# Doubling levels of triangular inverses computed on two diagonal halves, with the level masks moved to GpSimd

## The reference

```python
def step(s, inp):
    r_t, w_t, k_t, v_t, kk_t, a_t = inp
    s_kk = jnp.einsum("bhvk,bhk->bhv", s, -kk_t)
    s = (s * w_t[:, :, None, :]
         + s_kk[..., None] * (kk_t * a_t)[:, :, None, :]
         + v_t[..., None] * k_t[:, :, None, :])
    y = jnp.einsum("bhvk,bhk->bhv", s, r_t)
    return s, y
```

## Time and profile before

| what | value |
|---|---|
| median of 3 runs | 2468.97 us (2467.76 to 2470.97) |
| the profiled execution: its time | 2468.69 us |
| the profiled execution: its span, first to last instruction | 2466.9 us |
| PE, DVE, ACT, POOL busy | 98%, 68%, 51%, 22% of the span |
| mean granted clock of TensorE | 0.993 of full speed |
| the levels, first copy of `p` to the last addition | 196.0 to 270.4 us of the span |

### The profile page before, as it was taken

How to read it: one execution, slowest core, us unless ns; L and a number is a source line. 1 busy time by engine, 2 the same in 40 slices (tenths; PEclk the granted TensorE clock), 3 DMA queues, 4 the chain that set the end, 5 groups by cost and what they waited for, 6 DMA issues and landing times.

```text
span 2466.9 us, 42599 instructions
## 1 busy us (share of the span) xinstructions
PE 2406.5 (98%) x16775; PEld 2183.0 (88%) x16775; DVE 1682.1 (68%) x3026; ACT 1261.8 (51%) x2689; POOL 541.0 (22%) x423
## 2 busy tenths in 40 slices
PE   7999999999999999999999999999999999999997
PEld 6888989998789999999888888789999999888886
DVE  4737345446669767887777556659776888777556
ACT  6542335445555544445555555545455455555554
POOL 3640224546178300000000002358500000000000
PEclk9999999999999999999999999999999999999999
DMA  5320145564145666666777665235666666787664
GB/s 179 121 87 17 36 153 169 188 188 143 49 156 171 186 181 194 195 195 193 241 245 224 195 211 151 90 113 168 183 187 185 195 193 193 227 247 237 195 199 145
DMA packets 148069, 421.00 MB, mean 171 GB/s; under 512 B 15904, under 2 KB 49056, under 8 KB 147488
## 3 DMA queue, kind: packets, MB, share of 16 engines
q1 hardware_dynamic: 144080, 405.34, 53.2%
q0 software_dynamic: 2192, 8.99, 1.0%
q10 hardware_dynamic: 1600, 3.96, 0.5%
HBM read 400.40 MB, written 17.83 MB: 170 GB/s over the span
## 4 chain that ended last, share of the span: by engine, by line
PE 92%; DVE 4%; ACT 2%; DMA 1%; issue 0%; POOL 0%; ACTq 0%; DVEq 0%
PE pb L436 91%; PE pb L445 1%; ACT arena L1135 1%; DVE arena L1618 1%; DVE arena L1621 0%; ACT L1135 0%; DVE arena L1767 0%; DMA raw<-in_vT 0%; DMA H<-in_x 0%; ACT hi L1123 0%; DVE H L1618 0%; DVE sm L1932 0%; DVE arena L2062 0%; DVE arena L1791 0%; DMA raw<-in_w_out 0%
## 5 line engine op out<-in xcount | busy, mean ns | idle before, releaser
L1123 ACT CAST hi<-raw 128x512 fp32r<-128x512 f32 x1402 | 819.2, 620 | 376.4 <-PE pb L436 192.5
L436 PE MATMUL pb<-HTh,hi 128*128 128x256 f32 (+1 forms) x2968 | 858.9, 289 | 2.6 <-POOL lo L2341 1.9
L436 PE MATMUL pb<-HTh,lo 128*128 128x256 f32 (+1 forms) x2968 | 842.2, 284 | 0.0
L436 PE MATMUL pb<-HTl,hi 128*128 128x256 f32 (+1 forms) x2968 | 842.2, 284 | 0.0
L2341 POOL TENSOR_TENSOR lo<-raw,hi 128x512 fp32r<-128x512 f32 x383 | 520.2, 1382 | 564.1 <-ACT hi L1123 564.1
L1628 DVE TENSOR_TENSOR lo<-raw,hi 128x1024 fp32r<-128x1024 f32 x464 | 565.3, 1218 | 85.7 <-ACT hi L1123 85.5
L436 PEld LDWEIGHTS pb<-HTh,hi 128*128 128x128 f32 x2968 | 569.7, 192 | 7.2 <-issue 2.7
L436 PEld LDWEIGHTS pb<-HTl,hi 128*128 128x128 f32 x2968 | 570.1, 192 | 0.9
L436 PEld LDWEIGHTS pb<-HTh,lo 128*128 128x128 f32 x2968 | 569.6, 192 | 0.0
L436 PE MATMUL pb<-hi,WH 128*128 128x512 f32 x1112 | 433.6, 390 | 4.3 <-DVE WL L2305 4.3
L436 PE MATMUL pb<-lo,WH 128*128 128x512 f32 x1112 | 433.2, 390 | 0.0
(11 more groups left out here) (196 smaller groups left out, 2166.0 us busy)
## 6 DMA issues: line engine op xcount, KB each, us to landing
raw<-in_uT SPq DMA_DIRECT2D x256, 512.0 KB, 3.6
raw<-in_vT SPq DMA_DIRECT2D x256, 512.0 KB, 4.2
raw<-in_w_ffn_in SPq DMA_DIRECT2D x44, 512.0 KB, 4.0
raw<-in_wq SPq DMA_DIRECT2D x32, 512.0 KB, 3.6
wk<-kept SPq DMA_DIRECT2D x128, 128.0 KB, 3.8
raw<-in_w_in SPq DMA_DIRECT2D x24, 512.0 KB, 3.8
raw<-in_w_ffn_out SPq DMA_DIRECT2D x22, 512.0 KB, 4.4
raw<-in_w_gate SPq DMA_DIRECT2D x16, 512.0 KB, 3.3
```

The source lines that it names most:

```text
L436: return e.matmul(o, l, r, start=start, stop=stop)
L1123: e.copy(u.hi[k], u.half[k]).then_inc(*s.up("hi", ("hi", g)))
```

## The change

For blocks 1 and 2 and levels 1 to 5 (`halved`), each matmul of 128x128 is replaced by two of 64x64 on the diagonal quarters. The bank index `q` then no longer stands for four heads but for a half (partitions 0 to 63 or 64 to 127) of all 8 heads, and the matmuls of the two halves alternate. ACT's copies and DVE's additions go by halves too: 64 partitions by 8x64 elements instead of 128 by 4x128. PE's order within a level becomes p, x_up, xt_up, each whole, with a wait for both copies of `p` ahead of `x_up`; this holds for all levels and blocks, the last level and block 0 too. The masks of blocks 1 and 2 go from DVE to POOL, which makes each as soon as both parts of `p` have been computed; POOL does them behind gate unit 7, in its program order. Level 6 and block 0 keep their matmuls, and block 0 its masks on DVE.

```diff
+    def part_of(self, i, lv, k, q):
+        if halved(i, lv):
+            return self.mat(i, k)[PAR[q], :, PAR[q]]
+        return self.mat(i, k)[:, 4 * q:4 * q + 4, :]
+
+    def bank_of(self, psum, i, lv, q):
+        if halved(i, lv):
+            return psum[PAR[q], :].rearrange("p (h t) -> p h t", h=8)
+        return self.heads(psum, BLK[i][1])
...
+def halved(i, lv):
+    return i > 0 and lv < 6
...
-    def level(i, lv):
+    def level_product(name, i, lv, banks, lhs, rhs):
+
         n = BLK[i][1]
-        final = lv == (3 if n == 16 else 6)
-        bk = (0, 1) if i == 1 else (2, 3)
-        for q in range(2):
-            emptied(bk[q])
-            w.wait_ge(*s.to("n", i, lv))
-            for k in range(4):
-                h = 4 * q + k
-                x = mm(PB[bk[q]][0:n, k * n:(k + 1) * n], m.mat(i, Nk)[:, h, :], m.mat(i, Xk)[:, h, :], True, True)
-            x.then_inc(*s.up("blocks_ps", ("p_ps", i, lv, q)))
-            free[bk[q]] = [("p", i, lv, q)]
...
+        if halved(i, lv):
+            for q in range(2):
+                emptied(banks[q])
+            for h in range(8):
+                for q in range(2):
+                    r = PAR[q]
+                    x = mm(PB[banks[q]][r, h * 64:h * 64 + 64], m.mat(i, lhs)[r, h, r], m.mat(i, rhs)[r, h, r], True, True)
+                    if h == 7:
+                        x.then_inc(*s.up("blocks_ps", (name + "_ps", i, lv, q)))
+                        free[banks[q]] = [(name, i, lv, q)]
+        else:
+            for q in range(2):
+                emptied(banks[q])
                 for k in range(4):
                     h = 4 * q + k
...
+    def level(i, lv):
+        final = lv == (6 if i else 3)
+        first, second = ((0, 1), (4, 5)) if i == 1 else ((2, 3), (6, 7))
+        w.wait_ge(*s.to("n", i, lv))
+        if lv > 1:
+            for q in range(2):
+                w.wait_ge(*s.to("x_up", i, lv - 1, q))
+        level_product("p", i, lv, first, Nk, Xk)
+        for q in range(2):
+            w.wait_ge(*s.to("p", i, lv, q))
+            if lv > 1:
+                w.wait_ge(*s.to("xt_up", i, lv - 1, q))
+        if not final:
+            level_product("x_up", i, lv, first, XTk, Pk)
+        level_product("xt_up", i, lv, second, Pk, XTk)
...
-            e.copy(m.mat(i, Pk)[:, 4 * q:4 * q + 4, :], m.heads(PB[b], n)).then_inc(*s.up("powers", ("p", i, lv, q)))
+            e.copy(m.part_of(i, lv, Pk, q), m.bank_of(PB[b], i, lv, q)).then_inc(*s.up("powers", ("p", i, lv, q)))
...
-        if not final:
+        if not final and i == 0:
             own()
             tt(m.mat(i, Nk), m.mat(i, MTk), m.mask("lvT", n, 8, (lv + 1) * 128), M).then_inc(*up("blocks", ("n", i, lv + 1)))
...
     for g in range(16):
         take("gate", g)
+        if g == 7:
+            for lv in range(1, 6):
+                for i in (1, 2):
+                    w.wait_ge(*s.to("p_ps", i, lv, 0))
+                    w.wait_ge(*s.to("p_ps", i, lv, 1))
+                    x = tt(m.mat(i, Nk), m.mat(i, MTk), m.mask("lvT", 128, 8, (lv + 1) * 128), M)
+                    x.then_inc(*s.up("masks", ("n", i, lv + 1)))
```

More of the change, by code:

```diff
@@ L649, in tensor @@
             row_tile(k // 3, k % 3, 6)
-    def level(i, lv):
+    def level_product(name, i, lv, banks, lhs, rhs):
         n = BLK[i][1]
-        final = lv == (3 if n == 16 else 6)
-        bk = (0, 1) if i == 1 else (2, 3)
-        for q in range(2):
-            emptied(bk[q])
-            w.wait_ge(*s.to("n", i, lv))
-            for k in range(4):
-                h = 4 * q + k
-                x = mm(PB[bk[q]][0:n, k * n:(k + 1) * n], m.mat(i, Nk)[:, h, :], m.mat(i, Xk)[:, h, :], True, True)
-            x.then_inc(*s.up("blocks_ps", ("p_ps", i, lv, q)))
-            free[bk[q]] = [("p", i, lv, q)]
[L663 to L671, removed]
-            if not final:
-                b2 = bk[q]
-                emptied(b2)
+        if halved(i, lv):
[11 more added lines that the diff above has]
+                emptied(banks[q])
@@ L675, in level @@
                 for k in range(4):
                     h = 4 * q + k
-                    x = mm(PB[b2][0:n, k * n:(k + 1) * n], m.mat(i, XTk)[:, h, :], m.mat(i, Pk)[:, h, :], True, True)
-                x.then_inc(*s.up("blocks_ps", ("x_up_ps", i, lv, q)))
-                free[b2] = [("x_up", i, lv, q)]
+                    x = mm(PB[banks[q]][0:n, k * n:(k + 1) * n], m.mat(i, lhs)[:, h, :], m.mat(i, rhs)[:, h, :], True, True)
+                x.then_inc(*s.up("blocks_ps", (name + "_ps", i, lv, q)))
@@ L1785, in level @@
         for q in range(2):
-            hs, b, b2 = slice(4 * q, 4 * q + 4), (4 if i == 1 else 6) + q, (0 if i == 1 else 2) + q
-            x, xt = m.mat(i, Xk)[:, hs, :], m.mat(i, XTk)[:, hs, :]
+            b, b2 = (4 if i == 1 else 6) + q, (0 if i == 1 else 2) + q
+            x, xt = m.part_of(i, lv, Xk, q), m.part_of(i, lv, XTk, q)
             if not final:
@@ L1790, in level @@
                 own()
-                tt(x, x, m.heads(PB[b2], n), A).then_inc(*up("blocks", ("x_up", i, lv, q)))
+                tt(x, x, m.bank_of(PB[b2], i, lv, q), A).then_inc(*up("blocks", ("x_up", i, lv, q)))
             w.wait_ge(*s.to("xt_up_ps", i, lv, q))
@@ L1794, in level @@
             done = [("n", i, lv + 1)] if final and q else []
-            tt(xt, xt, m.heads(PB[b], n), A).then_inc(*up("blocks", ("xt_up", i, lv, q), *done))
-        if not final:
+            tt(xt, xt, m.bank_of(PB[b], i, lv, q), A).then_inc(*up("blocks", ("xt_up", i, lv, q), *done))
+        if not final and i == 0:
             own()
```

## The result

The changed kernel takes 2485.32 us (median of 4 runs, 2482.45 to 2487.57) against 2469.97 us for the kernel before (4 runs, 2467.76 to 2471.66). The ratio is 1.0059, with a 95% interval of 1.0046 to 1.0071: slower by 0.6%. The forecast was 2469.4 us, and the range ended at 2476. The profiled execution took 2486.74 us, its span is 2484.9 us.

The account below looks back on a forecast made before the run. PE was taken to bound the stage, DVE second. Levels -5.4 us, form changes +0.7 and clock falls +5.5 made +0.8 on the profiled 2468.69 us: forecast 2469.4 us, range 2462 to 2476.

Parts of the forecast that it names:

- rival C: Levels 1 to 5: the clock stays down, 1.1 us per fall; nine falls give 2473.8 us, twelve 2477; chance 0.11.
- about five falls: In the level stage the clock falls about five times, 3.4 us each, +5.5 us; bounds none and twelve.
- the rest of the program keeps its length: Behind the level stage PE goes straight on, so only the stage's length matters; no term for anything behind it.
- price of a fall: In the levels PE works some two thirds of each 3.4 us at the low clock, so one costs 1.1 us.
- the sum: Level stage: pitch changes of levels 1 to 6 and form changes give -4.7 us, clock falls +5.5, together +0.8.
- argument against C: In levels 1 to 5, matmuls slowed by the low clock fill PE's waits, which speaks against the clock staying down.
- rival A: Levels 2 to 6: the clock holds, since no single wait is above 1.6 us; 2464.0 us; chance 0.16.
- Records of 64x64: PE's halved products in levels 1 to 5: 30 ns per record, 96 records per block's level, bounds 26 and 56 ns.
- rival D: Halved products: the halves don't overlap, 6.7 us per block and level, 25 us more in all, 2490 us; chance 0.04.
- block's level: Blocks 1 and 2: 4.23 us of PE instead of 5.41, of which 1.35 are a wait; two copies 1.07 us.
- hold-up: Level 1: POOL's first mask delays DVE's preparation of block 2 from 201.2 to 203.6 us; bounds 0 and 3.5 us.
- rival B: Level 1: POOL's first mask waits for DVE instead of delaying it, 2.4 us less, 2467.0 us; chance 0.09.

Follow-up runs that it names:

- e1_filler: Changed kernel with idle 128x256 matmuls in PE's waits (ahead of x_up, block 0's products and block 2's first mask): 2470.57 us, 1.0013 of the kernel before.
- f1_filler_late_mask: e1_filler, with POOL's first mask also waiting until DVE has prepared block 2: 2469.45 us, 1.0003 of the kernel before.
- front runs: Kernel before with 480, 240 and 960 idle matmuls on 16 columns at its very front: 2488.4, 2475.4 and 2502.0 us, one run each.
- f2: Changed kernel, no fillers, first POOL mask late, from level 2 on other blocks' products between a block's p and x_up: 2462.15 us, 0.9970 of the kernel before.

## Why the prediction was wrong

The mechanism that decided is the prediction's rival C, given 0.11: the clock stays down. The forecast said "I expect about five falls, each as long as that one"; there were eleven. That is the step that failed. Why eleven and not five, the runs leave open in part: idle matmuls in the waits took ten of the falls away, but the forecast counted by the waits, and the falls go by place: but for level 1's long wait each begins at block 0's narrow matmuls. In the changed kernel the clock then stayed down through the next blocks' 64x64 matmuls, for two to four falls on end; level 5, with waits of 1.3 us and no level of block 0 ahead of it, has none. A second step failed beside it, outside the stage: that the rest of the program keeps its length. Point by point:

- **The price of a fall was right**: 1.1 us predicted, 1.05 measured by e1_filler. Six falls more than expected are 6.3 us of the 8.4 by which the stage is longer than the 75.2 us that the sum makes for it (74.4 - 4.7 + 5.5).
- **The argument against C was half right.** The argument against C, that slowed matmuls fill the waits, is borne out by the rows, but it only brings the clock back. With the clock the waits are back too, and it falls again in the next level. So C's price is right for this kernel, 2469.4 + 6 x 1.1 = 2476.0, though its picture, one long fall, is only half so: there were four stretches of two to four falls each.
- **The rule of the Trainium skill** that I weighed ("TensorE: Matmul & The Clock Gate", section "Why this matters for your kernels") would have given rival A. The fall at 204.8 us, in the wait of 3.6 us of level 1, fits it. The others it doesn't cover: in levels 2 to 5 no wait of PE was above 1.4 us, and the clock was at 0.50 for 28.7 us of them. The same page's section "A second HAM failure mode: psum-queue depth-cycling" tells of short idle times between groups of matmuls that make the clock go back and forth. The trace has both, the short idle times (15 of them, 16.0 us) and the clock that comes and goes; I hadn't weighed it, and it would have raised C's chance.
- **Terms of the structure.** Records of 64x64 came at 29 ns, 30 taken (96 in 3.01 us, less one's own length of 0.27), and at 53 ns while the clock was at 0.50. So rival D is out. The mask took 2.35 us (2.4 taken), the additions 0.69. The pair of copies takes 1.19 us instead of 1.07, which makes a block's level 4.34 instead of 4.23 us, 1.1 us over the ten. The hold-up was 2.0 us (2.4 taken), so rival B is out. f1_filler_late_mask, with no fall and no hold-up, has a stage of 71.5 us where the prediction's terms make 67.3 (74.4 - 4.7 - 2.4). Of the difference 2.0 are the overrun of the fillers, 1.1 the copies, and 1.1 are left, which no run parts.
- **What was never in the sum**: the 6.7 us behind the stage. "PE goes straight on behind it" took for granted that the rest of the program keeps its length. At the one transfer PE waits 2.0 us longer. Set side by side by ACT's casts, the two traces differ by 2.5 us between 370 and 588 us of before, where the clock of the changed kernel fell twice and that of before never, and by 5.2 us between 1440 and 1559, where the 2.0 us lie and two more falls; between 1582 and 1660 the changed kernel is 1.6 us shorter, with one fall less. The front runs show that the lengthening as a whole needs no halves; how much of it is the clock was read, not tested.
- **What was ahead of the stage**, 2.15 us of the profiled execution, is chance and isn't in the medians' difference to this size: 15.35 us between medians against 18.0 between spans.

Together: 8.4 in the stage, 6.7 behind and 2.15 ahead make the 17.2 us by which the profiled execution missed 2469.5. Even without what lies outside the stage, the time would have been 2477.9 us, beyond the range.

## What to carry to other kernels

Halving PE's work in a stage of short, dependent products may gain nothing as long as the order leaves PE waiting for each copy: first give PE another block's product to do in the wait (f2: 83.6 to 57.5 us of stage), then shrink the products. Where a stage repeats short waits and narrow matmuls level by level, reckon with a clock that falls again and again, and not only where the longest wait stands; count the falls in a trace, since here neither the waits nor their length told their number. A part that costs in one order (masks on POOL, -3.1 us) may be what carries the gain in another (+13.2 us), so undo parts in the order that you mean to keep.

## What the runs showed of the hardware

- TensorE's clock can fall to 1.2 GHz with no long wait near. Behind 205.2 us no wait of PE was above 1.4 us, and the granted clock was 0.50 in stretches of 6.9, 10.2 and 13.7 us; between the first two of them PE was busy for 3.91 of 6.8 us. With idle matmuls on the whole array in the same waits it fell once for 3.4 us, and in f1 never. It did not fall in level 5, with waits of the same 1.3 us. It stayed at 0.50 over 5.00 us in which PE ran 64x64 matmuls without a wait. In f2 it fell in levels 3 to 5 with no wait above 0.6 us. In the eleven kernels of the table 21 of 24 stretches at 0.50 begin at block 0's narrow matmuls or within 2.2 us behind them. So the narrow form may count beside the waits; no run parts the two.
- The four records on 64x64 quarters that replace one 128x128 matmul take 4 x 29 = 116 ns, where that matmul takes 225 (24 of them in the 5.41 us between two copies). Records on 64 columns that do not go by turns to two parts of the array, the 16x16 ones with 64 columns between 242.2 and 243.0 us of the kernel before, start 56 ns apart. So the two halves overlap almost wholly.
- A GpSimd and a VectorE instruction that both read two operands from SBUF shut each other out: the later one waits until the earlier one is over. 1.22 became 3.26 us, 2.35 became 3.21. The Trainium skill, "GPSIMD Engine Reference", section "Specifications", says that the two share their SBUF interfaces in that case. The trace agrees; here the wait lasts to the end of the other's instruction.
- Work on one engine can lengthen a stage far behind it: with 480 idle matmuls at the front a transfer at 1475 us took 1.6 us more (9.34 instead of 7.72 us) and the time behind the stage 5.7 us more, in a single run. The packets of the instruction queue rose with it, from 134 to 138; that these are the cause is not shown.
